# RWKV chunk outputs and state additions as one product of 128 rows each, with values and keys copied to the other partition half

## The reference, cut to what matters

```python
def _rwkv7_step(state, inp):
    r_t, w_t, k_t, v_t, a_t, b_t = inp
    sa = jnp.einsum('bhvk,bhk->bhv', state, a_t)
    state = (state * w_t[:, :, None, :] + sa[..., None] * b_t[:, :, None, :]
             + v_t[..., None] * k_t[:, :, None, :])
    return state, jnp.einsum('bhvk,bhk->bhv', state, r_t)
```

## Time and profile before

| | |
|---|---|
| median of 3 runs | 1279.96 us (1275.58 to 1284.19) |
| the profiled execution | 1278.47 us |
| its span in the trace | 1276.7 us |
| granted TensorE clock, mean | 0.969 |
| TensorE busy | 1163.9 us (91%) |
| VectorE / ScalarE / GpSimd busy | 711.7 / 266.8 / 92.4 us |
| HBM read | 244.80 MB |
| first transpose of tile 0 to first w_ro matmul | 943.8 to 1049.7 us |

### The profile page before, as it was taken

The page is one execution under the profiler, slowest core; times in us unless marked ns, Lnnn a source line. Parts: engine busy times, 40 slices in busy tenths (PEclk is TensorE's granted clock), DMA queues, the critical chain, the costliest instruction groups (busy, mean ns, idle before and its releaser), DMA issues.

```text
span 1276.7 us, 19693 instructions
## 1 busy us (share of the span) xinstructions
PE 1163.9 (91%) x8383; PEld 840.6 (66%) x8383; DVE 711.7 (56%) x1161; ACT 266.8 (21%) x467; POOL 92.4 (7%) x86
## 2 busy tenths in 40 slices
PE   6999999899877777999999999999998889999997
PEld 5855654556533433898478888766758774788886
DVE  5547421313212111775587777677884557887774
ACT  5413201221000001534110000326344221000000
POOL 2010000010000000120000000000110532000000
PEclk9999999898988888999999999999999999999999
DMA  9653135176999999532965561325300318655600
GB/s 344 221 193 132 66 119 210 66 273 271 421 421 418 420 421 410 205 145 81 312 208 176 193 198 66 97 98 185 107 2 4 124 36 277 229 178 185 198 1 33
DMA packets 106496, 247.21 MB, mean 194 GB/s; under 512 B 7121, under 2 KB 61408, under 8 KB 93986
## 3 DMA queue, kind: packets, MB, share of 16 engines
q1 hardware_dynamic: 106212, 245.71, 52.8%
q0 software_dynamic: 144, 0.15, 0.0%
q10 hardware_dynamic: 46, 0.01, 0.0%
HBM read 244.80 MB, written 1.05 MB: 193 GB/s over the span
## 4 chain that ended last, share of the span: by engine, by line
PE 82%; DMA 8%; DVE 4%; SPq 2%; ACT 2%; issue 2%; POOL 0%; DVEq 0%
PE bank L484 14%; PE bank L486 14%; PE bank L485 14%; PE bank L349 9%; DMA arena<-expert_w_gate 8%; PE bank L335 6%; PE bank L1352 4%; PE bank L1367 2%; PE bank L2470 2%; SPq L305 1%; PE bank L2451 1%; PE bank L2345 1%; PE bank L468 1%; PE bank L1403 1%; PE bank L1794 1%
## 5 line engine op out<-in xcount | busy, mean ns | idle before, releaser
L484 PE MATMUL bank<-work_rounded,work_rounded 128*128 128x512 f32 (+2 forms) x704 | 275.8, 392 | 8.9 <-DVE work_rounded L1728 5.2
L486 PE MATMUL bank<-work_rounded,work_rounded 128*128 128x512 f32 (+2 forms) x704 | 271.1, 385 | 0.0
L485 PE MATMUL bank<-ring_w_rounded,work_rounded 128*128 128x512 f32 (+2 forms) x576 | 222.2, 386 | 0.0
L484 PEld LDWEIGHTS bank<-work_rounded,work_rounded 128*128 128x128 f32 x704 | 132.2, 188 | 34.8 <-issue 5.7
L486 PEld LDWEIGHTS bank<-work_rounded,work_rounded 128*128 128x128 f32 x704 | 132.2, 188 | 24.5
L485 PEld LDWEIGHTS bank<-ring_w_rounded,work_rounded 128*128 128x128 f32 x576 | 109.1, 189 | 18.6 <-issue 0.2
L349 PE MATMUL bank<-arena 128*128 128x512 f32 x256 | 112.1, 594 | 3.1 <-ACT arena L1153 1.4
L1352 PE MATMUL bank<-arena 128*32 128x256 f32 x896 | 71.1, 439 | 45.1 <-DMA arena<-expert_w_gate 36.7
L1246 ACT ACTIVATE arena<-bank 128x256 f32<-128x256 f32 x52 | 20.0, 384 | 417.6 <-PE bank L486 336.5
L1728 DVE TENSOR_TENSOR ring_w_rounded<-arena,work_rounded 128x1024 fp32r<-128x1024 f32 x84 | 102.9, 1225 | 2.9
L1727 DVE CAST work_rounded<-arena 128x1024 fp32r<-128x1024 f32 (+1 forms) x140 | 93.8, 670 | 0.3
(11 more groups left out here) (420 smaller groups left out, 1676.5 us busy)
## 6 DMA issues: line engine op xcount, KB each, us to landing
arena<-expert_w_up SPq DMA_DIRECT2D x29, 1024.0 KB, 21.6
arena<-expert_w_down SPq DMA_DIRECT2D x28, 1024.0 KB, 26.4
arena<-expert_w_gate SPq DMA_DIRECT2D x27, 1024.0 KB, 17.2
arena<-ffn_w_gate SPq DMA_DIRECT2D x22, 1024.0 KB, 5.4
arena<-ffn_w_up SPq DMA_DIRECT2D x22, 1024.0 KB, 8.0
arena<-ffn_w_down SPq DMA_DIRECT2D x22, 1024.0 KB, 5.2
arena<-hy_w_in SPq DMA_DIRECT2D x12, 856.0 KB, 12.5
arena<-w_in SPq DMA_DIRECT2D x8, 1024.0 KB, 13.5
```

Of the source, the lines that this page charges most:

```text
L484: nc.tensor.matmul(out, lhsT[0], rhs[0], start=first, stop=False)
L485: nc.tensor.matmul(out, lhsT[0], rhs[1], start=False, stop=False)
L486: return nc.tensor.matmul(out, lhsT[1], rhs[0], start=False, stop=last)
```

## The change

y and Z become one product each, over all 128 partitions: the left side holds (a.r) of a chunk in that chunk's half and (k.r) in the other half, the right side (UV[c]) has u in the chunk's half and the values in the other. For Z the left side is BKEY[t][c], with a in the chunk's half and k in the other. To get there,

- rwmask's middle slots trade places, and products_pe writes the k products to the other half (slots: a.s, k.s, then a.r with k.r of chunk 0, then of chunk 1);
- ScalarE issues transfers from SBUF to SBUF of 64 partitions x 1024 columns (256 KB each): per tile two of values and four of keys, semaphore "swapped" (16 each). Values of tile 0 go ahead of the first turn, keys of tile 0 ahead of its chunks; all six of tile 1 behind chunks 0, once Z1.0.1 is filled;
- Mv is taken out of the inverse start and made after level 0 (values_pe), from the swapped values, behind a wait for 2 transfers (tile 0) or all 12 (tile 1);
- UG's copy becomes three: u of each half into UV (64 partitions x 256), g into UG (128 x 256);
- in chunks_pe both halves' HW products come first, then a wait for 6 (tile 0) or 12 transfers, then y and Z; VectorE's moves follow that order.

```diff
-    parts["rwmask"] = np.concatenate([-1.0 * strict_c, incl_c, strict_c, incl_c], 1).astype(float)
+    parts["rwmask"] = np.concatenate([-1.0 * strict_c, strict_c, incl_c, incl_c], 1).astype(float)
...
-        UG = RB[:, 4096:6144].rearrange("p (h n) -> p h n", h=RH)
+        UG = RB[:, 4096:5120].rearrange("p (h n) -> p h n", h=RH)
+        UV = [x.rearrange("p (h n) -> p h n", h=RH) for x in (RB[:, 5120:6144], work[:, 22528:23552])]
+        BKEY = [[x.rearrange("p (h n) -> p h n", h=RH) for x in (first, work[:, 3072:4096])]
+                for first in (R0[:, 3072:4096], s_[:, 0])]
...
-                                o = 256 * q + P * j
-                                mm = nc.tensor.matmul(pair[par][w, o:o + P].rearrange("p (x n) -> p x n", x=2),
-                                                      BK[t][p, 2 * g + q, j, w], AR[t][p, 2 * g + q, :, w],
-                                                      start=True, stop=True)
+                                c = HALVES.index(w)
+                                to = HALVES[1 - c] if j else w
+                                four = pair[par][to, 256 * q:256 * q + 256].rearrange("p (x n) -> p x n", x=4)
+                                mm = nc.tensor.matmul(four[:, j:3 + c:2 + c - j], BK[t][p, 2 * g + q, j, w],
+                                                      AR[t][p, 2 * g + q, :, w], start=True, stop=True)
...
-                blocks_pe(pe, "A", "Mv", t, half, lambda w, h: NM[t][w, h, 2 * CH:3 * CH],
-                          lambda w, h: v_[w, t, h * HD:(h + 1) * HD])
...
+        def values_pe(pe, t):
+
+            pe.wait_ge(sem("swapped"), (32, 192)[t])
+            for half in range(2):
+                ps = fill(pe, "A", f"Mv.{t}.{half}")
+                for i in range(8):
+                    h = 8 * half + i
+                    for c, w in enumerate(HALVES):
+                        other = HALVES[1 - c]
+                        mm = nc.tensor.matmul(ps[w, i * HD:(i + 1) * HD], NM[t][other, h, CH:2 * CH], UV[c][other, h],
+                                              start=True, stop=True)
+                mm.then_inc(full["A"], 1)
...
-                    for w in HALVES:
-                        nc.tensor.matmul(ps[w, o], NM[t][w, h, CH:2 * CH], UG[w, h, 0:HD], start=True, stop=False)
-                    for w in HALVES:
-                        mm = nc.tensor.matmul(ps[w, o], NM[t][w, h, 3 * CH:], tok(v_, w, h), start=False, stop=True)
...
+            pe.wait_ge(sem("swapped"), 96 * (t + 1))
+            for half in range(2):
+                ps = fill(pe, "A", f"y.{t}.{half}")
+                for i in range(8):
+                    h = 8 * half + i
+                    for c, w in enumerate(HALVES):
+                        mm = nc.tensor.matmul(ps[w, i * HD:(i + 1) * HD], NM[t][:, h, (2 + c) * CH:(3 + c) * CH], UV[c][:, h],
+                                              start=True, stop=True)
...
-                            nc.tensor.matmul(pair[c][p, q * HD:(q + 1) * HD], tok(a_, w, h), UG[w, h, 0:HD],
-                                             start=True, stop=False)
...
-                            mm = nc.tensor.matmul(pair[c][p, q * HD:(q + 1) * HD], tok(k_, w, h), tok(v_, w, h),
-                                                  start=False, stop=True)
+                            mm = nc.tensor.matmul(pair[c][p, q * HD:(q + 1) * HD], BKEY[t][c][:, h], UV[c][:, h],
+                                                  start=True, stop=True)
...
+            swapped_values_act(act, 0)
             turn_act(act, 0)
...
             turn_act(act, 1)
+            swapped_keys_act(act, 0)
             chunks_act(act, 0)
+            peek(act, "Z1.0.1")
+            swapped_values_act(act, 1)
+            swapped_keys_act(act, 1)
             inverse_start_act(act, 1)
...
+        def swapped_values_act(act, t):
+
+            await_moved(act, "w_rv.1.1")
+            for c, w in enumerate(HALVES):
+                act.dma_start(flat(UV[c][HALVES[1 - c]]), v_[w, t]).then_inc(sem("swapped"), 16)
+
+        def swapped_keys_act(act, t):
+
+            peek(act, f"NM.{1}.3.1")
+            for c, w in enumerate(HALVES):
+                act.dma_start(flat(BKEY[t][c][w]), a_[w, t]).then_inc(sem("swapped"), 16)
+                act.dma_start(flat(BKEY[t][c][HALVES[1 - c]]), k_[w, t]).then_inc(sem("swapped"), 16)
...
-                nc.scalar.copy(flat(UG[:, 4 * g:4 * g + 4]), ps[:, :]).then_inc(moved["A"], 1)
+                u, both = slice(4 * g, 4 * g + 4), ps[:, :].rearrange("p (h b n) -> p h b n", h=4, b=2)
+                for c, w in enumerate(HALVES):
+                    nc.scalar.copy(UV[c][w, u], both[w, :, 0])
+                nc.scalar.copy(UG[:, u], both[:, :, 1]).then_inc(moved["A"], 1)
```

More of the change, by code:

```diff
@@ L2513, in chunks_pe @@
                 await_moved(pe, f"UG.{t}.{2 * half + 1}")
-                ps = fill(pe, "A", f"y.{t}.{half}")
-                for i in range(8):
-                    h = 8 * half + i
-                    o = slice(i * HD, (i + 1) * HD)
-                    for w in HALVES:
-                        nc.tensor.matmul(ps[w, o], NM[t][w, h, CH:2 * CH], UG[w, h, 0:HD], start=True, stop=False)
-                    for w in HALVES:
-                        mm = nc.tensor.matmul(ps[w, o], NM[t][w, h, 3 * CH:], tok(v_, w, h), start=False, stop=True)
-                mm.then_inc(full["A"], 1)
                 pair = [fill(pe, "D", f"HW{c}.{t}.{half}") for c in range(2)]
@@ L2881, in chunks_dve @@
                     V.tensor_tensor(WZ[:, c, q4, 0:HD], v[:, :, HD:], bc(C("eye2"), 4, 1), ALU.add).then_inc(moved["D"], 1)
+            for half in range(2):
+                q4 = slice(4 * half, 4 * half + 4)
                 for c in range(2):
```

27 lines of the change are left out of this document (17 added, 10 removed).

## The result

The changed kernel takes 1293.63 us (median of 4 runs, 1291.62 to 1295.16) beside 1278.08 us of the kernel before (4 runs, 1275.58 to 1284.19): a ratio of 1.0106, 95% interval 1.0077 to 1.0136. That is 0.8 to 1.4% slower, above the whole range that was forecast.

A forecast was written before the change was run, and what follows sets the result against it. TensorE was taken as the bound, short of time for small matmuls and of instructions in a 106 us RWKV stretch. Terms 0.8 + 0.3 + 1.9 - 1.1 + 0.7 - 2.3 gave +0.3 us, forecast 1280.0, range 1274.5 to 1286.5.

The forecast's parts named there:

- The likeliest case: RWKV stretch from first transposes of tile 0 to first w_ro product: terms sum to +0.3 us, 1280.0 us; chance 0.52.
- C: Mv of tile 0, moved from before X2 to after level 0: its 64 matmul records have no cover, +1.9 us.
- D: Chunks of tile 0: wide products -1.95 us, a wait for ScalarE's copies +0.8; taken -1.1, from -2.0 to +2.
- E: Start of tile 1: Mv waits for all twelve transfers, there at 1006.4; +0.7 us, bounds -1.8 to +3.5.
- A: Values of tile 0: two DMA issues on ScalarE before its first turn copies hold up TensorE and VectorE, +0.8 us.
- B: Products in new slot order, neighbouring pairs on the same array quarter: 0 to +1.3 us, taken as +0.3.
- F: Chunks of tile 1: wide products -1.95 us, copies keep pace, 0.35 less waiting after the last Z; -2.3 us.
- the rival in which wide products do not overlap: y and Z of both tiles: each 128x64 record holds the array for 54 ns; +6.6 us, 1286.6; chance 0.07.
- The drain at a switch: Tiling switches around each tile's y and Z: at most 0.8 us in all by the skill's rule, nothing put in the sum.
- Transfers land late: Rival: y of tile 0 and Mv of tile 1 wait for ScalarE's transfers; +5.6 us together, 1285.9; chance 0.18.
- the prediction's own signs: Forecast wrong if the RWKV stretch is under 102 or over 110 us; DMA waits over 3 us would mean the transfers.
- Instruction supply decides: Rival: TensorE waits for instruction blocks, y and Z save two blocks, -7.6 us; -4.6 net, 1275.4; chance 0.19.

The follow-up runs named there:

- e2: Changed kernel plus three dummy 128x512 products in the gap before the second X2 of tile 0, Mv still late: 1291.48 us, ratio 1.0099 to before.
- e3: Kernel before with nothing changed but Mv of both tiles moved behind level 0: 1284.6 us, ratio 1.0037 to before.
- e1: Changed kernel with Mv of tile 0 back ahead of X2: 1289.63 us, ratio 1.0085 to before.
- e4: Changed kernel with all twelve transfers issued by SP instead of ScalarE, tile 1's ahead of the first w_ro load: 1287.8 us, ratio 1.006 to before.
- e7: Changed kernel with the edits of e1, e4 and e5 together: 1279.38 us, ratio 1.0000 to before.
- e8: e7 with two of tile 0's key transfers sent earlier, behind level 0 of tile 0: 1278.67 us, ratio 1.0001 to before.
- e13: Changed kernel with only the w_ro loads held for the first UG product of tile 1: 1287.61 us, ratio 1.0049 to before.
- e5: Changed kernel with a separate semaphore for values, so Mv of tile 1 waits for two transfers, not twelve: 1288.59 us, ratio 1.0077 to before.
- e11: Kernel before with only the w_ro loads held for the first UG product of tile 1: 1281.5 us, ratio 1.0012 to before.
- e12: e10 with g of each UG group copied ahead of u, with its own semaphore for HW: 1276.68 us, ratio 0.9972 to before.
- e10: e8 with all four w_ro loads held for the first UG product of tile 1: 1277.06 us, ratio 0.9972 to before.

## Why the prediction was wrong, point by point

The likeliest case said +0.3 us over the stretch; it was +10.5 in the profile, and 15.6 between the medians (13.5 by the ratio, 9.8 to 17.4 by its interval). The failed steps are the terms C, D and E, which were summed to +1.5 us and came to +11.4: the hole that Mv left was not priced, the transfers' issues were costed at half of what they take, and the transfers themselves at more than twice their pace. The wide products, which were meant to save, did so, a little less than reckoned.

**C, Mv of tile 0: forecast +1.9, measured +4.2.** That its 64 records "have no cover: +1.9" was right in mechanism and size (1.7, e2). What failed is the half of the step that was not asked. Taking Mv away from 955.61 leaves TensorE with nothing while it waits for VectorE's masks of the second half (the timeline of TensorE has "issue" there; VectorE writes the last of them, L2899, at 958.95 for 0.69 us, and TensorE starts at 959.74): 2.70 us of idle, after which the clock was at half for 6.7 us. The text had that very mechanism among its rows (2.3 us idle followed by 0.50) and used it only for transfers. e3 gives the loss on the kernel before alone, e1 takes stage C's part of it away, e2 takes the clock's part away while Mv stays late. Shown.

**D, chunks of tile 0: forecast -1.1, measured +1.5.** TensorE's busy time fell by 1.4 us (11.1 to 9.7), and 2.9 us of waits for ScalarE came in. Three sizes were off, the mechanism held. An issue on ScalarE was costed at 0.43 us, from one on SP; four in a row took 0.47, 0.61, 0.63 and 1.27, so 3.0 us and not 1.7 (SP showed the same growth in e4: 0.46, 0.60, 0.62, 1.24). The trace of before had a sign of it: of SP's five issues of L2709, the fourth took 0.43 us like the one quoted, and the fifth 0.74:

```profile
L2709 SPq DMA_DIRECT2D arena<-rw_ln_b x1: 739/739/739, 875.0 to 875.0; - x1
```

A copy of 256 columns was costed as half of one of 512, 0.29; this is the timeline of ScalarE in after:

```profile
998.53 0.37 ACT L2719 COPY arena<-bank 128x256 f32<-128x256 f32 x1
998.80 0.74 ACT L2718 COPY arena<-bank 64x256 f32<-64x256 f32 x2
```

Each takes 0.37, those of 64 partitions as well, so a group is 1.03 us and not 0.87, and TensorE fills banks faster than ScalarE empties them. TensorE waited 1.94 + 0.94 us for it where 0.8 was forecast. The keys, "within the cover if the early figure holds", were not within it: their last landing is 7.6 us after the first issue in e4. In after it came at 1002.20, after 7.5 us, and y started at 1003.06, so that this wait is hidden behind ScalarE's; with ScalarE freed it shows (e4, e7: 11.8), and with two keys left it is gone (e8: 10.3). Shown.

**E, start of tile 1: forecast +0.7, measured +5.8.** The sum let the twelve transfers land at 1006.4, 9 us after Z of tile 0, from 397 GB/s. They landed at 1021.08, 14.0 us after the first of six issues at 1007.06. Two errors add: the issues take 5.2 us and not 2.6, and the transfers do not move at 397 GB/s. Even with no load beside them the 1.5 MB need 9.6 us from the first issue to the last landing (e13; 10.2 in e4), where 6.4 were reckoned for 2.5 MB; beside the w_ro load the last transfer alone takes 9.89 us. Until the issues end no X2 is copied, so TensorE idled 3.90 us, and 3.4 us at half clock began with its next products; then it waited 2.7 us for the DMA, where 2 was forecast. e5 (no wait for the keys: -2.8 in E), e4 (no ScalarE issues: -2.4) and e7 (both: -8.1) split it. Shown. The w_ro load's own share is what e13 takes away: with w_ro late and all else as in after, the last landing comes 4.4 us sooner after the first issue, TensorE no longer waits for it, and E is 2.9 us shorter. Holding only the first w_ro back until the transfers are in was not tried.

**A and B, forecast +0.8 and +0.3.** A shows +0.8, but by luck: it is the half clock, not the issues. With the same length of half clock there, the kernels with ScalarE's two issues (e1, e2, e5, e13: 7.62 to 7.71 us) and those without (e3, e11, e12: 7.66 to 7.69) are alike. B is nil, with C at 12.44 in e1 as in before: 32 records of products take 1.12 us, 1.10 before. The chain of after:

```profile
950.66 1.12 PE bank L2448 x30
```

**F, chunks of tile 1: forecast -2.3, measured -1.4.** The tiles are close to the forecast: in tile 0 of after the y and Z halves took 1.08, 0.93, 0.93 and 0.96 us where 0.94 was reckoned, so the rival in which wide products do not overlap is dead, and in F TensorE's busy time fell by 1.9 us. The missing 0.9 is ScalarE again, for which TensorE waited 0.8 us ahead of the second HW half. That "the copies keep pace" was wrong: twelve of them from 1046.14 to 1050.35 are 4.2 us, where the UG products took 3.49.

**The drain at a switch, forecast 0.** The Trainium skill, "TensorEngine Tiling (Array Packing)", section "Key Properties", says a change of tiling mode drains TensorE. The trace agrees, and leaving it out of the sum was a small error. The prediction looked for an idle entry and found none, but the profile draws each of these records 0.22 us long, far over the start of the next, so a pause of 0.1 us leaves no idle time. The starts show it. The timeline of after, from the first y of tile 0 to X2 of tile 1:

```profile
1003.06 1.15 PE L2548 MATMUL bank<-arena 128*64 128x64 f32 x32
1004.04 1.10 PE L2556 MATMUL bank<-arena 128*64 128x64 f32 x32
1004.98 1.10 PE L2548 MATMUL bank<-arena 128*64 128x64 f32 x32
...
1006.94 2.08 PE L2458 MATMUL bank<-const,arena 64*64 64x64 f32 x64
```

From Z to y and from y to Z, both 128x64, 32 records take 0.93 or 0.94 us from start to start. The first y half, behind the switch, takes 0.98, the HW half ahead of it 1.03 (1002.03 to 1003.06), and the last Z half ahead of the switch back 1.03 (1005.91 to 1006.94). That is some 0.25 us in a tile, over half of what e12's 1.55 us lack to the 1.95 of the forecast, and within the "at most" 0.8 us for four switches that the prediction worked out from the rule.

**The rivals.** "Transfers land late" was right for Mv of tile 1 (2.7 us) and, once ScalarE is out of the way, for y of tile 0 (1.4 us in e4), and was too cheap: 1285.9 against 1293.6. Its price left out ScalarE's own lateness, and the clock behind Mv's gap. By the prediction's own signs the stretch of 116.4 us, over 110, would be the transfers if the DMA waits were over 3 us; they were 2.7, and most of the time went elsewhere. "Instruction supply decides" was no account of the result, but it explains why the repaired kernel wins so little. In e7 the transfers, issues and Mv are paid for, 512 records are gone, and the ratio is 1.0000: D +0.7, E -2.4, F -1.4, L1 +2.6. The saving of one stage was spent in the stalls of the next and in the half clock beside them. Only with the loads moved as well did 0.3% remain (e10). The Trainium skill, "Runtime: NRT & Kernel Launch", section "Instruction fetch mechanics", has it that fetch is hidden behind dispatch. By that rule neither e8's stalls of 2.3 and 3.6 us nor e11's of 3.13 beside a load should be. That these stalls are instruction fetch stays an inference, from their even spacing, the small transfers ahead of them and their growth beside large loads. No record names it.

**Left open.** The profile of after is 14.5 us longer than that of before, of which the stretch holds 10.5. Some 1.9 lie ahead of 945.7 us and 2.1 behind the first w_ro product, in code that the change does not touch. Both are within what executions differ by: the first transpose starts between 939.6 and 948.0 us, and the part behind the first w_ro product takes 226.9 to 229.1 us, while before's own two profiles have the first transpose at 943.8 and 948.0. What sets these is not known. In medians, what e1, e4 and e5 win back covers the whole loss.

## What to carry to other kernels

When work is moved off a spot where an engine waits, price the hole it leaves as well as the place it goes to: on TensorE an idle piece of 2.7 us among small products was followed by 3.4 to 6.7 us at half clock, which cost 1.5 to 2.5 us more. A transfer's issue takes time of the engine that issues it, and more within a burst, so give a burst of issues to an engine that nobody waits for, and let each consumer wait for its own transfers alone. A gain in a stage that is fed by the same supply as the next one (here instructions beside weight loads) has to be measured at the end of both.

## What the hardware showed that was not expected

- A transfer from SBUF to SBUF of 64 partitions x 4 KB (256 KB) landed 4.8 (e13) to 6.3 us (e8) after its issue when last of four or six with no large load issued ahead of it, and 9.2 (e2) to 10.1 us (e1) with a 1 MB load beside it; 1 MB took 7.6 us from its first issue with the DMA otherwise nearly idle (e4), 0.14 MB per us.
- The issue of such a transfer grew within a burst of four, from 0.47 to 1.27 us on ScalarE (after) and from 0.46 to 1.24 on SP (e4); in bursts of six one took up to 1.85 us (e13).
- A switch between 64x64 and 128x64 products cost TensorE about 0.1 us without an idle entry in the profile (after).
- A copy from PSUM by ScalarE of 64 partitions x 256 took the 0.37 us of one of 128 x 256, and the 128 x 512 one 0.58.
- With three useless products of 128x512 in a gap of 2.7 us the granted clock stayed at 1.00 and that stage was 2.5 us shorter (e2), with no gain for the kernel that can be measured.
- One edit that delays 4 MB of loads gained 0.3 and 0.6% on two kernels (e8 to e10, after to e13) and nothing that can be measured on a third (before to e11).
